# Sample attention laid between the query matmuls, the choice of experts and the last tile's queries behind it, the one-hot rows last

## The reference

```python
# sample sequences: 8 of them, 4 new tokens each, 2048 cached positions in 16 pages of 128
s = einsum('bqhc,bkc->bhqk', q_lat, ckv) + einsum('bqhr,bkr->bhqk', q_rope, kpe)   # 8 heads
p = softmax(s * SM_SCALE, axis=-1)
o = einsum('bhqk,bkc->bqhc', p, ckv)                                               # latent output
...
h = layer_norm(ALPHA * h + mixer_output(o, ...))
# product-key expert retrieval, 544 or so tokens, 8 heads, 2 x 128 sub keys, 16384 experts
q = einsum('nd,de->ne', x, w_pq)              # 16 blocks of 128 query columns
s = einsum('nhpc,hpkc->nhpk', q, sub_keys)
sv, si = top_k(s, 16)                         # per half
cv, ci = top_k(all sums of two halves, 16)    # per head: the 16 experts and their softmax gates
y = sum over chosen experts of gate * gelu(u_e . x) * v_e
```

## Time and profile before

| | |
|---|---|
| time before, median of 3 runs | 2213.6 us (2201.3 to 2216.74) |
| the profiled execution | 2203.03 us, of which span 2200.9 us |
| PE / DVE / ACT / POOL busy share of the span | 91% / 66% / 31% / 13% |
| instructions | 28283 |

### The profile page before, as it was taken

The page is one execution under the profiler, slowest core; times in us unless marked ns, Lnnn a source line. Parts: engine busy times, 40 slices in busy tenths (PEclk is TensorE's granted clock), DMA queues, the critical chain, the costliest instruction groups (busy, mean ns, idle before and its releaser), DMA issues. The chain is left out here.

```text
span 2200.9 us, 28283 instructions
## 1 busy us (share of the span) xinstructions
PE 2007.9 (91%) x9569; PEld 1625.7 (74%) x9569; DVE 1446.4 (66%) x3102; ACT 690.6 (31%) x1152; POOL 276.7 (13%) x229
## 2 busy tenths in 40 slices
PE   6998899569999898679899999999999999999996
PEld 3445556465456888559788888898999999999995
DVE  3001442544257888866788787777668888888888
ACT  1013332421012010546533333343333333333332
POOL 0000000001000110000122121112112222232230
PEclk9999588668998555799999999999999999999998
DMA  5210002025022431235887767778788898998992
GB/s 184 75 62 7 1 1 77 1 81 207 25 77 65 130 99 44 95 153 230 341 296 254 258 242 260 254 276 304 255 321 321 336 356 322 344 345 322 355 334 108
DMA packets 133914, 430.23 MB, mean 195 GB/s; under 512 B 12257, under 2 KB 70034, under 8 KB 109938
## 3 DMA queue, kind: packets, MB, share of 16 engines
q1 hardware_dynamic: 107730, 252.10, 32.1%
q0 software_dynamic: 26112, 177.22, 21.4%
HBM read 396.92 MB, written 31.97 MB: 195 GB/s over the span
## 5 line engine op out<-in xcount | busy, mean ns | idle before, releaser
L1315 POOL DMA_INDIRECT hi<-euv,lo x160 | 241.3, 1508 | 1067.2 <-DVE hi L1783 816.3
L976 PE MATMUL ps<-xh,ul 128*128 128x384 f32 x1024 | 346.9, 339 | 0.0
L976 PE MATMUL ps<-xl,uh 128*128 128x384 f32 x1024 | 345.8, 338 | 0.0
L976 PE MATMUL ps<-xh,uh 128*128 128x384 f32 x1024 | 343.8, 336 | 0.0
L987 PE MATMUL ps<-vh,hh 128*128 128x512 f32 x768 | 244.6, 400 | 24.2 <-DVE hl L1724 24.0
L1019 ACT ACTIVATE hi<-ps 128x512 f32<-128x512 f32 (+12 forms) x288 | 172.2, 649 | 253.6 <-PE ps L949 54.4
L987 PE MATMUL ps<-vh,hl 128*128 128x512 f32 x768 | 240.7, 395 | 0.0
L987 PE MATMUL ps<-vl,hh 128*128 128x512 f32 x768 | 239.3, 393 | 0.0
L1712 DVE TENSOR_TENSOR ul<-lo,uh 128x1024 fp32r<-128x1024 f32 x128 | 156.2, 1221 | 86.9 <-ACT uh L1019 86.9
L1783 DVE SCALAR_TENSOR_TENSOR hi<-hi,lo 128x1024 f32<-128x1024 f32 x160 | 198.5, 1282 | 6.8
L1019 ACT ACTIVATE vh<-lo 128x1024 fp32r<-128x1024 f32 x128 | 135.4, 1058 | 196.0 <-PE ps L987 184.5
(11 more groups left out here) (307 smaller groups left out, 2740.3 us busy)
## 6 DMA issues: line engine op xcount, KB each, us to landing
lo<-eu SPq DMA_DIRECT2D x128, 512.0 KB, 7.5
lo<-ev SPq DMA_DIRECT2D x128, 512.0 KB, 6.0
gates<-hi SPq DMA_DIRECT2D x6, 4096.0 KB, 11.9
hi<-gates SPq DMA_DIRECT2D x62, 384.0 KB, 6.9
hi<-w_pq SPq DMA_DIRECT2D x8, 2048.0 KB, 9.6
hi<-w_in SPq DMA_DIRECT2D x5, 2048.0 KB, 9.0
hi<-cache SPq DMA_DIRECT2D x64, 144.0 KB, 2.7
hi<-cache POOLq DMA_DIRECT2D x64, 144.0 KB, 2.9
```

What stands on the lines that cost most here:

```text
L976: last = nc.tensor.matmul(ps[:, 6 + p, 0:ND * TD], a[p][:, k * 128:(k + 1) * 128], b[:, k, :], start=(k == 0 and b is xh and a is uh), sto ...
L1315: nc.gpsimd.indirect_dma_start(ring[slot].rearrange("p a d -> p (a d)"), None, euv, bass.IndirectOffsetOnAxis(at, 0)).then_inc(r_in[slot], 16)
```

## The change

Nothing is computed that was not computed before, and nothing is left out. The order is another one:

- PE: sequence `b` of the attention and query blocks `2b` and `2b + 1` form one group. The choice of PSUM banks follows: one bank for the attention's scores, sums and values each, two for queries instead of four, one for key scores instead of two.
- The pages have two sets of buffers instead of three: pages of sequence `b + 1` are loaded once `sm_values(b - 1)` is done.
- DVE takes `best_keys` two blocks and two tiles at a time (`ranks`) between the attention steps. All of `choice` follows the attention.
- PE's last-tile work (projection, 16 query blocks, keys) stands in one piece behind the attention, ahead of the one-hot matmuls; the loads of its weights move up on SP's list. The one-hot rows are no longer interrupted.

The core of the diff:

```diff
-            for b in range(2 * PH):                      # PE: all 16 query blocks ...
-                ...8 matmuls of 448 columns...
-                if b >= 1:
-                    keys(b - 1)
-            keys(2 * PH - 1)
...
             sm_keys(0)
-            sm_keys(1)
-            sm_scores(0)
             for b in range(SB):                          # PE: ... and the 8 sequences
+                sm_scores(b)
+                queries(2 * b, 0, KD)
+                sm_turn(b)
+                queries(2 * b + 1, 0, KD // 2)
+                sm_spread(b)
+                queries(2 * b + 1, KD // 2, KD)
+                keys(2 * b)
                 if b + 1 < SB:
-                    sm_scores(b + 1)
-                else:
-                    sm_turn(b)
-                    sm_spread(b)
+                    sm_keys(b + 1)
                 sm_values(b)
+                keys(2 * b + 1)
...
+            hidden_transposes(TI + ST)                   # PE: the last tile, ahead of the one-hots
+            pe.wait_ge(s["ht_done"], TI + TI)
+            for b in range(2 * PH):
+                tail_queries(b)
+                if b >= 1:
+                    tail_keys(b - 1)
+            tail_keys(2 * PH - 1)
```

```diff
             for b in range(SB):                          # ACT
+                query_copy(2 * b)
+                query_copy(2 * b + 1)
+                score_copy(2 * b)
+                if b + 1 < SB:
+                    sm_rows(b + 1)
                 act.wait_ge(s["sm_sub"], b + 1)
                 ...two exponentials...
-                if b + 2 < SB:
-                    sm_rows(b + 2)
-                    sm_keys(b + 2)
+                if b + 1 < SB:
+                    sm_keys(b + 1)
+                score_copy(2 * b + 1)
```

```diff
-            for b in range(SB):                          # DVE
-                sm_max(b)
-                sm_diag(b)
-                sm_shift(b)
-                for part in range(2):
-                    choice(b // 2, 2 * (b % 2) + part)
-                sm_out(b)
+            for b in range(SB + 1):
+                if b < SB:
+                    sm_max(b)
+                if b >= 1:
+                    sm_out(b - 1)
+                    dve.wait_ge(s["sc_done"], 2 * b)
+                    ranks(2 * b - 2, 0)
+                if b < SB:
+                    sm_diag(b)
+                if b >= 1:
+                    ranks(2 * b - 2, 2)
+                if b < SB:
+                    sm_shift(b)
+            for t in range(ND + 1):
+                for part in range(4):
+                    choice(t, part)
+                if t == 0:
+                    dve.wait_ge(s["ln1_in"], 64)
+                    residual(ST, 1, ln1b)
```

More of the change, by code:

```diff
@@ L350, in build @@
         r_in = [s[f"r_in{n}"] for n in range(RING)]
-        c_in, d_in = [s[f"c_in{n}"] for n in range(3)], [s[f"d_in{n}"] for n in range(3)]
+        c_in, d_in = [s[f"c_in{n}"] for n in range(2)], [s[f"d_in{n}"] for n in range(2)]
         NJ = TI * NH
@@ L884, in sm_values @@
                                  skip_group_check=True)
                 for k in range(PAGES):
-                    if k == HP and b + 2 < SB:
-                        sm_keys(b + 2)
-                    nc.tensor.matmul(ps[:, 4 + b % 2, 0:NS], page(b, k)[:, 0:KVR], p[:, k, :], start=(k == 0), stop=False)
-                nc.tensor.matmul(ps[:, 4 + b % 2, 0:NS], zs, p[0:NS, PAGES, :],
+                    nc.tensor.matmul(ps[:, 6, 0:NS], page(b, k)[:, 0:KVR], p[:, k, :], start=(k == 0), stop=False)
@@ L939, in tail_keys @@
                 nc.tensor.matmul(ps[:, 6, 0:NK], pqT[:, b % 2, 0:128], skT[:, b, :], start=True, stop=True).then_inc(s["sc_ps"], 1)
+            pe.wait_ge(s["xm_done"], 13)
+            for n in range(2):
+                pe.wait_ge(pq_in[n], 48)
+                for k in range(KD):
+                    last = nc.tensor.matmul(ps[0:TR, 4 + n, :], xmb[:, k, :], wob[n][:, k, :], start=(k == 0), stop=(k == KD - 1))
+                last.then_inc(s["wo_ps"], 1)
+            hidden_transposes(TI + ST)
+            pe.wait_ge(s["ht_done"], TI + TI)
+            for b in range(2 * PH):
+                tail_queries(b)
+                if b >= 1:
+                    tail_keys(b - 1)
+            tail_keys(2 * PH - 1)
             for g in range(ND * TD // 4):
@@ L951, in _ @@
                 last.then_inc(s["gm_ps"], 1)
-                if g in (26, 32):
-                    n = (g - 26) // 6
-                    pe.wait_ge(s["xm_done"], 13)
-                    pe.wait_ge(pq_in[n], 48)
-                    for k in range(KD):
-                        last = nc.tensor.matmul(ps[0:TR, 4 + n, :], xmb[:, k, :], wob[n][:, k, :], start=(k == 0), stop=(k == KD - 1))
-                    last.then_inc(s["wo_ps"], 1)
-                if g == 43:
-                    pe.wait_ge(s["tr_done"], 2)
-                    hidden_transposes(TI + ST)
-                    pe.wait_ge(s["ht_done"], TI + TI)
-                if g >= 45 and g % 2 and g < 79:
-                    b = (g - 45) // 2
-                    if b < 2 * PH:
-                        tail_queries(b)
-                    if b >= 1:
-                        tail_keys(b - 1)
             def up(p, n_u, n_free):
@@ L1153, in score_copy @@
                 ins.then_inc(s["sc_done"], 1)
-            for b in range(2 * PH):
-                query_copy(b)
-                if b >= 1:
-                    score_copy(b - 1)
-            score_copy(2 * PH - 1)
             def softmax_exp(i):
@@ L1176, in sm_keys @@
                     act.wait_ge(s["sm_s"], b - 1)
-                copy(kT[b % 2].rearrange("p a k -> p (a k)"), ps[:, 2, :]).then_inc(s["sm_kc"], 1)
-            for b in range(2):
-                sm_rows(b)
-                sm_keys(b)
+                copy(kT[b % 2].rearrange("p a k -> p (a k)"), ps[:, 4, :]).then_inc(s["sm_kc"], 1)
+            sm_rows(0)
+            sm_keys(0)
             for b in range(SB):
+                query_copy(2 * b)
[3 more added lines that the diff above has]
+                    sm_rows(b + 1)
                 act.wait_ge(s["sm_sub"], b + 1)
@@ L1196, in _ @@
                 copy(xmb[:, g, :], ps[:, 4 + g, 0:TR]).then_inc(s["xm_done"], 1)
-            copy(hTb[:, :, TR:128], hT[:, :, AT - MORE:AT])
             act.wait_ge(s["xm_ps"], 13)
             copy(xmb[:, 4:8, :], ps[:, 4, 0:MH * TR].rearrange("p (h t) -> p h t", h=MH)).then_inc(s["xm_done"], 1)
+            act.wait_ge(s["l1_done"], 1)
+            copy(hTb[:, :, TR:128], hT[:, :, AT - MORE:AT])
+            softmax_exp(0)
+            root(ST, TI + ST)
+            hidden_copies(TI + ST)
+            for b in range(2 * PH):
+                query_copy(2 * PH + b)
+                if b >= 1:
+                    score_copy(2 * PH + b - 1)
+                if b in (4, 12):
+                    softmax_exp(b // 4 if b == 4 else 2)
+            score_copy(4 * PH - 1)
+            softmax_exp(ND)
             def gates_copy(g):
```

185 lines of the change are left out of this document (76 added, 109 removed).

## The result

| | before | after |
|---|---|---|
| median of the runs | 2209.3 us (4 runs, 2201.3 to 2216.7) | 2246.9 us (4 runs, 2231.0 to 2253.4) |
| the profiled execution, and its span | 2203.0, 2200.9 | 2231.0, 2229.1 |

The ratio is 1.016, 95% interval 1.009 to 1.023: slower, by 37.6 us between the medians, which is under 2%. Over all eight runs its median is 2239.6, 32 us over the 2207.6 of before. The profiled execution was the fastest of its four.

The account below looks back on a forecast made before the run. PE was taken to bound queries and half-clock attention. Queries with attention 265, choice 120.3 and one-hot rows 144.6 sum to 530 against 490.2 us, 40 slower: 2243 or 2254, given as 2250, range 2205 to 2300.

Parts of the forecast that it names:

- The bound and the cause: Ahead of the expert loop: PE bounds queries and half-clock attention; the choice of experts on DVE loses its cover.
- Piece B: The choice of experts alone on DVE, with the last tile's residual: 120.3 us, covering the last tile's PE work.
- Piece C: The one-hot rows alone: 134.7 us of DVE work, 1.9 for ACT, 8 for PE's cold starts; 144.6, bounds 136.6 and 150.
- Piece A: Queries with attention, from 582 to DVE's last ranks: 265 us, bounds 229 and 327.
- The disputed term: Clock loss in queries with attention: 4.5 us per sequence, 36 in all, from narrow page matmuls and neighbouring work at half clock.
- The first: Rival: the clock holds through the narrow stretches; queries with attention 229, sum 494, +4, 2217 us; chance 0.17.
- The second: Rival: all attention stays at half clock and each group's queries begin there; +102, 2316 us; chance 0.10.
- The third: Rival: faster, clock holds and no PE wait before `sm_keys`; queries with attention 215, about -23, 2190 us; chance 0.08.
- The fourth: Rival: the last tile's projection, loads and queries take more than 120 us beside the choice; about 2265 us; chance 0.05.
- The other rule for the clock: Skill's rule applied to the groups: longest wait about 1.7 us, so full clock kept and the sum 36 lower.

Follow-up runs that it names:

- fine mix: The kernel after with single dense query steps between quarters of the scores and values, one block first, DVE's ranks behind the shift: 2184.0 us, ratio 0.991.
- lumped kernel: The fine mix with its dense query steps in lumps again, orders of DVE and ACT unchanged: 2251.0 us, ratio 1.020 to before.
- narrow work split: The kernel after with each group reordered so that the narrow attention matmuls come in shorter pieces between dense query work: 2240.1 us, ratio 1.017 to before.

## Why the prediction was right, step by step

- **The bound and the cause.** Right. What the change costs is the DVE work that had lain under a PE at half clock. The earlier trace rows said it, and the kernel with only that moved shows it: +102. The prediction set 120 us of DVE work against 34 and 35 saved, which alone would give 51; its sum of 40 is right because the 12 us from 882 to the first one-hot row went too; most of them were PE's wait of 8.7 for `sm_out`.
- **Piece B**: 120.3 predicted, 119.8 measured, from the durations in the earlier trace rows. The work takes the same time alone. The tail was put at 80 to 100 us; it ended 79.6 after B's start.
- **Piece C**: 144.6 predicted, 139.4 measured. DVE's 134.7 of work were right (134.5 in the window); I charged 8 for PE's cold starts and they cost 4.8, and 1.9 for ACT, which cost 1.2.
- **Piece A**: 265 predicted, 252.2 and 264.4 measured. Its base held: 229 at full clock, of it 17 for new waits (14.5 measured); the two profiles less what their clock cost are 230.7 and 229.7. The disputed term, 36 for the clock, is 21.5 by the first profile (86 us at 0.75) and 34.7 by the second (124 us at 0.72), but its shape was wrong. I spread 4.5 us over each of eight sequences, with groups of 31 us; what happens is that the first three or five groups lose it, and the rest, at 27 us, lose nothing. Some 8 us of it in each profile, besides, are the start at half clock, of which the base held 2.4; the falls cost 13.6 and 27.3, not 36. It is also where a run of after differs from the next.
- **The total** was met in part by luck. The pieces were forecast at 530 and measured at 511.4 and 523.7, so against before they cost 21 and some 33 us and not 40. The medians came to 37.6 and, over all eight runs, 32; the loop, which I had at no change, was 8 and 6 us longer in the two pairs.
- **Rivals.** The first, that the clock holds, is what the later groups do, and the price I gave (229) is met by the fine mix and undercut (217), since it has almost no waits and its ranks end 7 us behind PE's last value matmul (795 to 802), not 11. The second, half clock in over half of the stretch, came true in none of these, though the lumped kernel comes near (105 of 229 us). The third, faster with A at 215, did not come true in after, but the fine mix has it: A at 217, and 23 us under before. The fourth, the tail as the bound, had 40 us to spare.
- **The expert loop** was to keep its length. The four profiles of both kernels can't tell (1084 to 1094 before, 1090 to 1102 after).
- **The other rule for the clock.** By the rule of the Trainium skill, TensorE: Matmul & The Clock Gate, section Why this matters for your kernels, that the clock is kept where no long idle gap lies between bursts of matmuls, the sum would have been 36 lower. Pieces A of 252 and 264 against 229 lie with the rows, and the lumped kernel shows falls with PE never idle.

Open is why the clock, once it held through one group of after, held through all the later ones, while the lumped kernel, whose groups have nearly the same lumps, lost it again and again (0.70 to 0.94 in all six stretches). The runs here show it and do not explain it.

## What to carry to other kernels

Before moving work out from under a slow engine, price it as if it stood alone on its own engine, and ask what will then be idle: here the three moves were +102, -31 and -40, and only their sum counted. Where narrow matmuls share PE with dense ones, try to mix them step by step and not block by block; here the same work in the same total order of stages took 217 us mixed and 264 in lumps. And in a stretch with a fixed amount of work on one engine (some 361 us of DVE here, in every kernel), read the order by that engine's idle time. It says no more than the stretch's length, from which it is worked out, but it says how much is left to win: 102 to 235 us here, in nearly the order of the medians.

## What the runs showed of the hardware that I had not expected

- Page matmuls of 32 columns, at 0.50 for 180 us without dense work around them, ran at 1.00 with dense steps of 0.9 us between quarters of them: 204 us without one fall.
- The clock fell without waiting: PE busy for 28.00 of 28 us at a mean clock of 0.70 (lumped).
- A fall can land on the dense work behind the narrow piece and not on the piece: a block of 7.98 us against 6.28 (narrow work split).
- The same kernel was below full clock in its first three groups in one execution and in its first five in another, 12 us apart.
- The expert loop, with the same code in all of these kernels, took from 1082 to 1102 us.
